# Two-layer hybrid attention, mLSTM and MoE kernel: the last two expert rounds go back to tokens by products in the array

## The reference

```python
def moe(h, router_w, router_b, w1, w3, w2):
    ...                                  # two experts per token, chosen within one group of four
    gates = jnp.sum(jax.nn.one_hot(idx, N_EXPERTS, dtype=jnp.float32) * wsel[..., None], axis=1)
    a = jnp.einsum('nd,edf->nef', t, w1)
    b = jnp.einsum('nd,edf->nef', t, w3)
    hid = jax.nn.silu(a) * b * gates[..., None].astype(t.dtype)
    return jnp.einsum('nef,efd->nd', hid, w2).reshape(B, L, D)

    x = x + g1x * (jnp.concatenate([mla_x, ml_x, na_x], axis=-1) @ w_out)
    x = x + g2x * moe(rmsnorm(x, norm2_g) * (1 + sc2x) + sh2x, router_w, ...)
```

## Time and profile before

| what | value |
|---|---|
| median of 3 runs | 1096.32 us |
| the profiled execution | 1098.64 us, of which 1096.5 us is its span (first to last instruction) |
| instructions | 12148 |
| PE busy | 940.1 us (86% of the span) |
| DVE busy | 443.0 us (40%) |
| ACT busy | 270.4 us (25%) |
| POOL busy | 173.7 us (16%) |
| mean granted TensorE clock | 0.925 of full |
| DMA | 208.51 MB, 190 GB/s |

### The profile page before, as it was taken

The page is one execution under the profiler, slowest core; times in us unless marked ns, Lnnn a source line. Parts: engine busy times, 40 slices in busy tenths (PEclk is TensorE's granted clock), DMA queues, the critical chain, the costliest instruction groups (busy, mean ns, idle before and its releaser), DMA issues.

```text
span 1096.5 us, 12148 instructions
## 1 busy us (share of the span) xinstructions
PE 940.1 (86%) x4283; PEld 523.7 (48%) x4283; DVE 443.0 (40%) x1109; ACT 270.4 (25%) x642; POOL 173.7 (16%) x210
## 2 busy tenths in 40 slices
PE   2699989989979998799999926999998698798782
PEld 0365454655566446454454414747664563533220
DVE  0306653575876244212121135166467652411113
ACT  0301213334544113121111112031345340211100
POOL 3441110111000001211212006002011100211100
PEclk9799988898989989899999977999899899699886
DMA  7972222466700105558887761432376017589963
GB/s 247 351 168 94 77 77 77 155 243 232 293 1 2 39 1 223 206 222 320 317 334 296 263 229 39 156 107 77 129 257 229 1 64 291 223 331 416 417 256 148
DMA packets 69153, 208.51 MB, mean 190 GB/s; under 512 B 10737, under 2 KB 19209, under 8 KB 59876
## 3 DMA queue, kind: packets, MB, share of 16 engines
q1 hardware_dynamic: 56864, 181.51, 44.4%
q0 software_dynamic: 9328, 16.66, 5.1%
q10 hardware_dynamic: 2900, 9.53, 2.3%
HBM read 201.04 MB, written 18.69 MB: 200 GB/s over the span
## 4 chain that ended last, share of the span: by engine, by line
PE 77%; DVE 10%; DMA 4%; issue 4%; ACT 2%; POOL 2%; ACTq 1%; SPq 0%; DVEq 0%; POOLq 0%
PE bank L1832 16%; PE bank L1538 10%; PE bank L1742 8%; PE bank L1856 8%; PE bank L1448 7%; PE bank L1526 7%; PE bank L1686 3%; PE bank L1619 3%; PE bank L1495 3%; PE bank L1597 2%; PE bank L1707 2%; POOL ST L1073 2%; DMA BRANCH<-in_w_mod 1%; PE bank L1605 1%; PE bank L1807 1%
## 5 line engine op out<-in xcount | busy, mean ns | idle before, releaser
L1832 PE MATMUL bank<-RINGW,NA 128*128 128x512 f32 (+1 forms) x448 | 174.6, 607 | 18.9 <-issue 15.8
L1073 POOL TENSOR_TENSOR ST<-ST,RT 128x1 f32<-128x1 f32 (+4 forms) x46 | 51.5, 1119 | 477.4 <-DVE ST L1963 226.5
L1832 PEld LDWEIGHTS bank<-RINGW,NA 128*128 128x128 f32 (+1 forms) x448 | 68.9, 170 | 118.5 <-issue 118.5
L1538 PE MATMUL bank<-RINGW,H 128*128 128x512 f32 (+4 forms) x384 | 119.0, 470 | 0.0
L2453 DVE SCALAR_TENSOR_TENSOR BRANCH<-BRANCH,bank 128x256 f32<-128x256 f32 x24 | 10.1, 422 | 216.2 <-ACT BRANCH L1392 216.2
L1538 PEld LDWEIGHTS bank<-RINGW,H 128*128 128x128 f32 x384 | 68.7, 190 | 49.4 <-issue 45.6
L1742 PE MATMUL bank<-RINGW,H 128*128 128x512 f32 x192 | 86.1, 610 | 0.0
L1526 PE MATMUL bank<-H,RINGW 128*128 128x512 f32 (+1 forms) x192 | 75.0, 550 | 2.7 <-ACT H L1192 2.7
L1448 PE MATMUL bank<-IDENT,WORK 128*128 128x128 f32 (+1 forms) x244 | 35.3, 294 | 36.0 <-DVE WORK L1965 34.8
L1129 POOL DMA_INDIRECT pairs<-BRANCH,IDX x24 | 24.1, 1004 | 255.9 <-ACT BRANCH L1412 237.9
L1742 PEld LDWEIGHTS bank<-RINGW,H 128*128 128x128 f32 x192 | 37.3, 196 | 46.0 <-issue 46.0
(11 more groups left out here) (295 smaller groups left out, 1390.4 us busy)
## 6 DMA issues: line engine op xcount, KB each, us to landing
RINGW<-in_moe_w SPq DMA_DIRECT2D x56, 1024.0 KB, 10.8
RINGW<-in_w_mod SPq DMA_DIRECT2D x23, 2048.0 KB, 8.0
W2R<-in_moe_w SPq DMA_DIRECT2D x15, 1024.0 KB, 5.2
PROJ<-in_moe_w SPq DMA_DIRECT2D x11, 1024.0 KB, 5.1
RINGW<-in_w_out SPq DMA_DIRECT2D x4, 2048.0 KB, 8.3
WORK<-in_moe_w SPq DMA_DIRECT2D x8, 1024.0 KB, 15.4
RINGW<-in_w_in SPq DMA_DIRECT2D x4, 1536.0 KB, 8.6
RINGW<-in_w_in SPq DMA_DIRECT2D x2, 2048.0 KB, 11.0
```

The lines of the kernel that those rows point to most:

```text
L1073: pool.tensor_tensor(r[:, 0:w], m[:, 0:w], POOL_HALF[:, 0:w], ALU.pow).then_inc(rstd_ready, 1)
L1538: ins = pe.matmul(bank_of(s)[:, 0:nn], HT[:, kk, t * P:(t + 1) * P], wv[:, kk, off:off + nn], start=kk == 0, stop=kk == KD - 1)
L1832: ins = pe.matmul(bank_of(s)[seats, :], XGT[n % 2][:, kk, seats], w[:, kk, :], start=kk == 0, stop=kk == KD - 1)
```

## The change

Layer 0's rounds 14 and 15 and layer 1's rounds 6 and 7 (`RETURN = (2, 2)`) are no longer scattered into `pairs`. For such a round `rseat` computes on DVE, for every token, which seat of the round it has; `rsend` spreads these numbers over the partitions (transposes, PE) and compares them with the seat's own number (DVE), which gives a 0/1 matrix `HOME` of seats x tokens; `ret` multiplies `HOME` with `YO` for each tile and half (PE) and DVE adds the product from PSUM to `X`. `pairs` is read back by SP's queue (`read_back`) as soon as the last scattered round has landed, and `comb` adds both parts straight to `X`. `pairs` must therefore hold zeros where nothing is scattered: POOL writes them (`zero_table`, eight DMAs of 512 KB in layer 0 and four in layer 1's `gates`). The gains are applied at the evacuation of `y`: both halves now on DVE, in layer 0 after one instruction of 1024 columns that mixes the two gain rows by a flag per seat (`TABS[:, e, 3:4]`), for which `gdiff` replaces the second row by the difference. `gbc2` stands ahead of `tot`. In the last layer each half of a tile goes to the output by itself.

```diff
@@ make_schedule @@
-        s += [("pfx", l, 1), ("oh", l, 1), ("tot", l)]
-        s += [("xT", l, 0), ("slots", l), ("xg", l, 1), ("xg", l, 2), ("ab", l, 0)]
+        s += [("pfx", l, 1), ("oh", l, 1), ("gbc2", l), ("tot", l)]
+        s += [("xT", l, 0), ("slots", l), ("xg", l, 1), ("xg", l, 2), ("gdiff", l), ("ab", l, 0)]
         s += [("yT", l, 0), ("xT", l, 1), ("y", l, 0), ("xg", l, 3), ("ys", l, 0)]
-        s += [("ab", l, 1), ("gbc2", l), ("xT", l, 2)]
+        s += [("ab", l, 1), ("xT", l, 2)]
...
         for e in range(1, nr):
...
             s += [("yT", l, e)]
+            s += [("ret", l, e - 1, t) for t in tq] if e - 1 >= sr else []
+            s += [("comb", l, t) for t in tq] if e == nr - 1 and RETURN[l] > 1 else []
             s += [("xT", l, e + 2)] if e + 2 < nr else []
             s += [("y", l, e)]
             s += [("xg", l, e + 3)] if e + 3 < nr else []
-            s += [("ys", l, e)]
+            s += [("ys", l, e)] if e < sr else []
+            s += first if swap else []
+            s += [("rsend", l, e + 1)] if sr <= e + 1 < nr else []
+            s += [("rseat", l, e + 2)] if sr <= e + 2 < nr else []
         s += [("dense", l)]
         for i, t in enumerate(tq):
-            s += [("comb", l, t), ("moe_out", l, t)]
+            s += [("comb", l, t)] if RETURN[l] == 1 else []
+            s += [("ret", l, nr - 1, t)]
@@ SP @@
+            def read_back(l):
+                sr = stored_rounds(l)
+                for e in (sr - 2, sr - 1):
+                    sp.wait_ge(ys_stored[(l * N_E + e) % 2], 16 * stored_n[(l, e)])
+                sp.wait_ge(*full_of(("xT", l, len(rounds(l)) - 1, 1)))
+                for t in tiles_q(l):
+                    p0, p1 = pair_home(l, t)
+                    sp.dma_start(p0, pairs[t * P:(t + 1) * P, :]).then_inc(pair_loaded[t], 16)
+                    sp.dma_start(p1, pairs[TOK + t * P:TOK + (t + 1) * P, :]).then_inc(pair_loaded[t], 16)
...
                 if p[0] == "w_u" and p[1]:
+                    read_back(p[1] - 1)
@@ POOL, gates @@
+            def zero_table(blocks):
+                zeros = N_R[:, 0:D]
+                link(pool.memset(zeros, 0.0))
+                for b in blocks:
+                    pool.dma_start(pairs[b * P:(b + 1) * P, :], zeros).then_inc(table_zero, 16)
...
                     if l == 0:
                         prepare_dram()
+                        zero_table(range(2 * T))
+                        pool.wait_ge(table_zero, 32 * T)
                     if l:
+                        for t in tiles_q(l - 1):
+                            pool.wait_ge(*pairs_in(l - 1, t))
+                        pool.wait_ge(*full_of(("ret", l - 1, len(rounds(l - 1)) - 1, tiles_q(l - 1)[-1], 1)))
+                        zero_table([c * T + t for c in (0, 1) for t in tiles_q(l)])
+                        pool.wait_ge(table_zero, 32 * T + 32 * len(tiles_q(l)))
                         pool.wait_ge(nmax_ready, max(UNIT_AT[u] for u in UNITS if u[1] == l - 1) + 1)
                     load_bias(l)
@@ PE @@
+                elif k == "rsend":
+                    pe.wait_ge(rseat_ready, rseat_n[("rseat",) + s[1:]])
+                    for c in (0, 1):
+                        open_bank(s + (c,))
+                        for i, t in enumerate(tq):
+                            o = 2 * T * (s[2] % 2) + 2 * t + c
+                            ins = pe.matmul(bank_of(s + (c,))[:, i * P:(i + 1) * P],
+                                            RSEAT[:, o:o + 1].broadcast_to([P, P]), IDENT[:, :], start=True, stop=True,
+                                            is_transpose=True)
+                        ins.then_inc(full_of(s + (c,))[0], 1)
+                elif k == "ret":
...
+                    pe.wait_ge(home_ready, rsend_n[("rsend", l, e)])
+                    for n in (0, 1):
+                        open_bank(s + (n,))
...
+                        pe.wait_ge(*free_of(("y", l, e, n)))
+                        pe.matmul(bank_of(s + (n,))[:, :], home_of(l, e, t), yo[:, 512 * n:512 * n + 512],
+                                  start=not by_products, stop=True).then_inc(full_of(s + (n,))[0], 1)
@@ DVE @@
+                elif k == "rsend":
...
+                    dve.tensor_scalar(out, bank_of(s + (0,))[:, 0:w], me, None, ALU.is_equal).then_inc(
+                        free_of(s + (0,))[0], 1)
...
+                    link(dve.scalar_tensor_tensor(out, bank_of(s + (1,))[:, 0:w], me, out, ALU.is_equal, ALU.add))
+                elif k == "ret":
...
+                        dve.tensor_tensor(xx, xx, bank_of(key)[:, :], ALU.add).then_inc(free_of(key)[0], 1)
                 elif k == "y":
-                        dve.tensor_copy(YO[n % 2][:, 0:512], bank_of(key)[:, :]).then_inc(free_of(key)[0], 1)
+                    if l < DEPTH - 1:
+                        link(dve.scalar_tensor_tensor(yo, GB[:, 1, :], TABS[:, e, 3:4], GB[:, 0, :], ALU.mult, ALU.add))
+                    for n in (0, 1):
...
+                            dve.tensor_tensor(yo[:, cols], bank_of(key)[:, :], gain, ALU.mult).then_inc(
+                                free_of(key)[0], 1)
                 elif k == "comb":
-                    link(dve.tensor_tensor(ACC[:, t, :], ACC[:, t, :], XS[:, t, :], ALU.add))
+                    link(dve.tensor_tensor(Xv[:, t, :], Xv[:, t, :], p1, ALU.add))
+                    if not (l < DEPTH - 1 and RETURN[l] == 1):
+                        link(dve.tensor_tensor(Xv[:, t, :], Xv[:, t, :], p0, ALU.add))
-                elif k == "moe_out":
...
-                    link(dve.tensor_tensor(ACC[:, t, :], ACC[:, t, :], GB[:, st, :], ALU.mult))
-                    ins = dve.tensor_tensor(Xv[:, t, :], Xv[:, t, :], ACC[:, t, :], ALU.add)
```

More of the change, by code:

```diff
@@ L59, with stored_rounds @@
 DIRECT = 1
+RETURN = (2, 2)
+def stored_rounds(l):
+    return len(rounds(l)) - RETURN[l]
 NOWHERE = 65536.0
@@ L436, in build @@
                 last_job_of_piece[("w2", l, e)] = st + (1,)
+        elif k in ("rsend", "ret"):
+            add(st + (0,))
+            add(st + (1,))
     job_at = {k: i for i, k in enumerate(jobs)}
@@ L746, in build, with yo_free, home_of, pair_home @@
         grid_key = {n: s for s, n in grid_n.items()}
+        rseat_n, rsend_n = order("rseat"), order("rsend")
+        yo_stored, stored_n = [0, 0], {}
+        for m in range(DEPTH):
+            for r in range(stored_rounds(m)):
+                yo_stored[(m * N_E + r) % 2] += 1
+                stored_n[(m, r)] = yo_stored[(m * N_E + r) % 2]
+        def yo_free(l, e):
+            if expert_n(l, e) < 2:
+                return None
+            l, e = expert_key(expert_n(l, e) - 2)
+            if e < stored_rounds(l):
+                return ys_stored[(l * N_E + e) % 2], 16 * stored_n[(l, e)]
+            return full_of(("ret", l, e, tiles_q(l)[-1], 1))
+        def home_of(l, e, t):
+            return HOME[l][e % 2][:, t - tiles_q(l)[0], :]
+        def pair_home(l, t):
+            if l < DEPTH - 1:
+                p0 = PR[:, 2048 + D * t:2048 + D * t + D] if t < 2 else N_R[:, D * t:D * t + D]
+                return p0, XS[:, t, :]
+            return XG[t - 2], (XG[2] if t == 2 else M[:, 4096:4096 + D])
+        def pairs_in(l, t):
+            return pair_loaded[t], 32 * sum(t in tiles_q(m) for m in range(l + 1))
         send_n = lambda l, st, r: sum(len(tiles_q(m)) // 2 for m in range(l)) * DIRECT + (
@@ L1308, in _ @@
                     t = s[2]
+                    act.wait_ge(table_zero, 32 * sum(len(tiles_q(m)) for m in range(l + 1)))
                     act.wait_ge(*full_of(s))
@@ L2411, in _ @@
                     dve.wait_ge(over_ready, l + 1)
+                    link(dve.tensor_scalar(NOTOVER[:, :], most, float(SEATS[l]), None, ALU.is_le))
                 elif k == "iota":
@@ L2415, in _ @@
                     dve.wait_ge(iota_ready, 1)
+                    for c in (0, 1):
+                        link(dve.memset(ENT[:, 2:4, c, 3], 1.0))
                     tick(dve, free_of(s)[0])
@@ L2461, in _ @@
                 elif k == "y":
[L2462 to L2472 removed]
+                    e = s[2]
```

146 lines of the change are left out of this document (88 added, 58 removed).

## The result

| | us, median (runs) | from - to |
|---|---|---|
| before, same comparison | 1096.78 (4) | 1094.52 - 1097.30 |
| changed | 1084.17 (4) | 1081.65 - 1086.37 |

The ratio is 0.9888 (95% interval 0.9861 to 0.9915): faster by 12.6 us. The forecast was 1090.0 with a range of 1085.5 to 1094.5; the time lies 1.3 us under it. The profiled run took 1081.65 us, its span is 1079.5.

A forecast was written before the change was run, and what follows sets the result against it. PE was taken to bound layer 0's rounds and weight loads layer 1's. Layer 0's +0.5 and layer 1's -7.0 gave -6.5 us from the median 1096.32, say 1090, range 1085.5 to 1094.5.

The forecast's parts named there:

- Zeroing the table: POOL's zero writes ahead of layer 0's `cnorm`: 20 to 27 us, all within its 28.5 us idle, so cost 0.
- Run noise of 1.4: Scatter between runs, in us, counted into the forecast's own spread of 1087.5 to 1092.5.
- Gain rows earlier: Moving `gbc2`'s 16 transposes out of layer 0's round 1 into an earlier PE wait saves 1.75 us.
- Evacuation: Some 2 us more DVE work per layer 0 round, hidden by PE: 0 in a steady round.
- The return of layer 0: Rounds 14 and 15 coming back by products: +2.0 us taken, between +1.2 and +2.9.
- the branch: A branch over `dense` on DVE's path in layer 0's return: 0.7 us taken, bounds 0 and 3.24.
- the give-back in `hT`: Layer 0's end: 16 transposes take 1.9 us instead of 3.61, since PE has worked before; up to 1.7 us back.
- the second memset: POOL clearing 1024 more columns in layer 1's `gates`: taken as 0, with +0.8 us kept in the range.
- Layer 1, -7.0: Rounds 6 and 7 returning by products end layer 1 7.0 us earlier, or 3.5 if products run at half clock.
- Rival 1: Layer 1's last `ab` keeps full clock after a shorter PE wait, saving 2.98 us more: 1086.8; chance 0.20.
- Rival 2: Return products at half clock in both layers, nothing given back in `hT`: -2.1 us together, 1094.2; chance 0.13.
- Rivals 3 and 4: Zeroing lands too late, about 1109, chance 0.04; DVE's branch and slower adds limit layer 1, 1093.9, chance 0.08.

The follow-up runs named there:

- b_wait3: The kernel before with only six memsets added ahead of DVE's gate rows in layer 0, a pure delay; mean 1089.0 us, ratio to before 0.9970.
- b_zero: The kernel before with only the zeroing of the table added, in both layers; 1098.15 us, ratio to before 1.0053.
- b_gbc2: The kernel before with only the gain rows' step moved ahead of the totals; 1097.75 us over 6 runs, too few and too wide for a ratio.
- a_again: The changed kernel, unchanged, compared once more; 1085.98 us over 12 runs, ratio to before 0.9962.
- b_same: The kernel before, word for word, run again for a second profile; 1094.71 us over 12 runs, ratio to before 1.0001.
- a_ret11: The changed kernel with only the last round of each layer, not the last two, returned by products; 1074.84 us, ratio to before 0.9831.

## Why the prediction was wrong

**The step that failed: "Zeroing the table ... Term 0."** I asked whether the delay of POOL is longer than its idle time ahead of `cnorm` (28.54 us in the earlier trace rows), and it is not. I did not ask on what POOL's work is moved. It went on top of DVE's gate rows, +4.6 us in this profile, and DVE's delay reaches PE as a pause of 6.2 instead of 3.0 us, behind which the half clock of layer 0's scores did not come: 7.3 us back. That a pure delay does this in part of the runs, and is worth 3.8 +-2.0 us, is shown by `b_wait3` and its two companions. For the zeroing's own delay only profiles speak: of the seven profiles with the early zeroing five have 0.91 or 1.00 from 180 to 200, two have 0.66 and 0.69; and `b_zero`, whose profile has 0.91, is slower than before over its runs. So the 0 had no ground: there is a loss of 4.6 us on DVE and a gain of clock behind it, and what the two come to, even in sign, stays open.

**Where the 13.7 us ahead of the first `ab` come from.** The last 12 products of the values start 0.5 us later; 7.3 us are saved up to the last of the rows shown; and 6.9 behind them. `b_wait3`, which has no part of the change, has 5.1 of these 6.9, of which 2.9 lie in the 32 records of L1742, again at the higher clock. Some 1.9 us are the change's own, a term that I did not have. It is mostly the routed product, 3.94 us instead of 5.58:

```profile
432.18 3.94 PE L1857 MATMUL bank<-BRANCH,WORK 128*128 128x128 f32 x32 [0.33 <-DVE BRANCH L2555]
```

It takes 3.8 to 4.0 us in all eleven profiles of kernels with the change, and 5.55 to 5.73 in all six without. `b_gbc2` had the pause ahead of it cut to 0.64 us and still took 5.72, so the moved gain rows alone do not do it; no run tested what does.

**Luck.** Some 12 of these 13.7 us are what this execution shares with the profile of `b_wait3`, beside a profile of before with the low clock at both places. Over all runs the change is worth 5.4 +-2.0 us, near the forecast's 6.5, but not by its terms. The measured median lies under the range since the first four runs of the changed kernel lie 4.1 us under the mean of its 28, and those of before 2.7 over the mean of its 114. Whether the three unprofiled ones of the four had the same early clock as the profiled one no trace shows.

**"Run noise of 1.4."** It was read from three runs within 2.8 us. The standard deviation of one program is 5.0, and the median 1096.32, from which the forecast was counted, lies 2.6 above the mean of 114 runs. The 0.3% that I said a measurement can tell falls with it. A range with this in it would have held the time.

**Gain rows earlier, -1.75.** -0.8: a longer wait for DVE, above. Together with `rsend` (0.9, as forecast) layer 0's rounds come out even.

**Evacuation, 0.** Right: no gap in PE, DVE 55.43 us of 145.

**The return of layer 0.** From `y` of round 14 to layer 1's first product +3.8, +2.5 and +1.8 us in three profiles of the changed kernel (`a_again` the last), +1.1 forecast. The pause of 9.6 us and the half clock behind it were right, and the branch is hidden by the wait for PE. Wrong were the give-back in `hT` (its last 16 transposes took 3.65 us after a pause of 3.04, no less than before's 3.61) and the second memset, priced at 0 with 0.8 as the other end: +0.9.

**Layer 1, -7.0.** -5.8, -4.3 and -5.7 in the three profiles, against 28.85 us in the mean of before's two. The sequence was as walked; the term was too large because the four return products ran half slow, 5.24 to 6.67 us for eight records where those of round 6 took 3.60, behind a pause of 3.12 us. That is the step to the lower bound (-3.5) that I had named.

**Rival 1** (the last `ab` at full clock) happened in this profile: 7.09 us. It is not the change's doing: `b_same` has 7.1 and `a_again` 8.8. Rival 2's slow returns came in part. Rivals 3 and 4 did not: the landing was 13 us, DVE's adds into `X` took the 0.69 us of the row, and its pause behind the branch (1.63 us) was a wait for PE.

What stays open is by what rule the chip grants the clock in the early part. With 3.0 us of pause it was low each time; with 3.6 us or more it was high in nine profiles of eleven; why, no run shows, and `a_ret11`'s 0.69 after 6.3 us contradicts a simple rule.
